# A squared-ReLU perceptron whose first matrix goes by seven quarter products in place of eight, in seven of eight feature groups

## The reference

```python
def squared_relu_mlp_2(h, w1, w2):
    return jnp.square(jax.nn.relu(h @ w1)) @ w2
...
        x = x + memory_xattn(rmsnorm(x, xa_ln[l]), rmsnorm(mem, xa_mem_ln[l]),
                             xa_wq[l], xa_wk[l], xa_wv[l], xa_wo[l])
        x = x + squared_relu_mlp_2(rmsnorm(x, ff_ln[l]), ff_w1[l], ff_w2[l])
```

## Time and profile before

| what | us |
|---|---|
| median of 3 runs (3623.42 to 3625.64) | 3624.16 |
| the profiled execution | 3652.24 |
| its span, first to last instruction | 3650.2 |
| PE busy in it | 3454.2 |
| DVE busy | 1768.0 |
| ACT busy | 1295.5 |

### The profile page before, as it was taken

One profiled execution on the slowest core, in us unless ns is written; L12 is line 12 of the kernel. 1 busy time (PEld: TensorE's weight loads), 2 busy tenths in 40 slices (PEclk: granted clock), 3 DMA queues, 4 the chain that ended last, 5 costly groups with the idle time before them and its releaser, 6 DMA issues. The chain is left out here.

```text
span 3650.2 us, 52599 instructions
## 1 busy us (share of the span) xinstructions
PE 3454.2 (95%) x21636; PEld 2817.0 (77%) x21636; DVE 1768.0 (48%) x2628; ACT 1295.5 (35%) x2096; POOL 159.2 (4%) x214
## 2 busy tenths in 40 slices
PE   7789899999999899999999989999999999999997
PEld 5687787788877587788877868788878767878886
DVE  5635653444444753444466354444452555444444
ACT  5223243322233743322234134432232574433221
POOL 0110000000000000000000200000000251000000
PEclk9899899999999999999999699999999999999998
DMA  3003131222231131222221023222232002222220
GB/s 145 23 4 108 59 137 51 89 96 99 93 107 58 40 134 56 91 96 92 92 83 54 2 81 116 70 85 100 92 119 75 36 2 94 104 78 96 92 92 35
DMA packets 42724, 289.78 MB, mean 79 GB/s; under 512 B 5475, under 2 KB 6243, under 8 KB 8860
## 3 DMA queue, kind: packets, MB, share of 16 engines
q1 hardware_dynamic: 42524, 286.92, 22.0%
HBM read 284.79 MB, written 2.12 MB: 79 GB/s over the span
## 5 line engine op out<-in xcount | busy, mean ns | idle before, releaser
L924 ACT ACTIVATE w_hi<-w_raw 128x2048 fp32r<-128x2048 f32 x112 | 214.8, 1918 | 861.6 <-PE ps L1044 445.7
L308 DVE TENSOR_TENSOR w_lo<-w_raw,w_hi 128x2048 fp32r<-128x2048 f32 x145 | 330.2, 2277 | 324.5 <-ACT w_hi L300 324.2
L1040 PE MATMUL ps<-a_x_hi,w_hi 128*128 128x512 f32 x1024 | 408.0, 398 | 7.5 <-PEq L270 7.5
L1041 PE MATMUL ps<-a_x_hi,w_lo 128*128 128x512 f32 x1024 | 405.7, 396 | 0.0
L1064 PE MATMUL ps<-mlp_u_lo,w_hi 128*128 128x512 f32 x1024 | 404.5, 395 | 0.0
L1065 PE MATMUL ps<-mlp_u_hi,w_lo 128*128 128x512 f32 x1024 | 404.5, 395 | 0.0
L1044 PE MATMUL ps<-a_x_lo,w_hi 128*128 128x512 f32 x1024 | 404.4, 395 | 0.0
L1063 PE MATMUL ps<-mlp_u_hi,w_hi 128*128 128x512 f32 x1024 | 404.4, 395 | 0.0
L414 PE MATMUL ps<-x_hi,w_hi 128*128 128x512 f32 x768 | 310.6, 404 | 24.4 <-PEq L270 17.0
L300 ACT ACTIVATE w_hi<-w_raw 128x2048 fp32r<-128x2048 f32 x145 | 274.9, 1896 | 96.5 <-PE ps L1065 41.0
L414 PE MATMUL ps<-x_hi,w_lo 128*128 128x512 f32 x768 | 308.3, 401 | 0.0
(11 more groups left out here) (568 smaller groups left out, 6121.6 us busy)
## 6 DMA issues: line engine op xcount, KB each, us to landing
w_raw<-in_weights SPq DMA_DIRECT2D x255, 1024.0 KB, 4.8
x_mem<-in_mem SPq DMA_DIRECT2D x4, 1024.0 KB, 4.9
hT<-in_x SPq DMA_DIRECT2D x1, 2048.0 KB
d_bias<-bias_rows SPq DMA_DIRECT2D x1, 2048.0 KB, 9.6
n_w<-in_cmp_w SPq DMA_DIRECT2D x1, 2048.0 KB, 7.5
out_h<-hT SPq DMA_DIRECT2D x1, 2048.0 KB, 6.3
t_xi<-in_ret_xi SPq DMA_DIRECT2D x1, 1024.0 KB, 7.2
w_raw<-in_weights SPq DMA_DIRECT2D x2, 512.0 KB, 3.3
```

The source lines that it names most:

```text
L308: dve.tensor_tensor(self.wlo[b % SPLIT][:, 0:width], self.raw[b % RAW][:, 0:width], self.whi[b % SPLIT][:, 0:width].bitcast(F32), ALU.subt ...
L924: act.activation(c.whi[b % SPLIT][:, :], c.raw[b % RAW][:, :], ACT.Copy).then_inc(c.hi_made.sem, 1)
L1040: pe.matmul(c.ps[:, t, :], whi[:, k, cols], x_hi[:, k, :], start=k == 0, stop=False)
L1041: pe.matmul(c.ps[:, t, :], wlo[:, k, cols], x_hi[:, k, :], start=False, stop=False)
```

## The change

For groups 1 to 7 the 512 x 1024 piece A of `w1` (transposed: features by k) and the 1024 x 512 tokens B are cut into 2 x 2 quarters: A into 256 features x 512 k, B into 512 k x 256 tokens. Before, the four quarters of the result took eight quarter products. Now they take seven (Strassen's algorithm in Winograd's form): of a11, a12 and a22, and of four sums of weight quarters (s1 = a21 + a22, s1 - a11 and so on), each with b11, b21, b22 or a difference of token quarters t1 to t4. A product is 2 tiles of 128 features x 4 k's x 3 = 24 matmuls of 256 tokens, both tiles in one bank.

- DVE makes the four sums of weight quarters (`mix`, L1153), 128x1024 each, mostly in place in `w_raw`. ACT and DVE then make hi and lo of each of the seven factors by half blocks (`step_part`, L1077 and L1161). The two blocks of a group held 4 halves; now there are 7.
- ACT copies the first product out of PSUM; DVE adds the products in seven additions of 128x512 (L1174), and relu (L1179) now reads SBUF, not PSUM.
- The token differences are made once in each perceptron (`MixedTokens`): ACT scales the 8 tiles of `hT`, DVE makes four differences, ACT and DVE their hi and lo parts. All of this is done while PE works on group 0's `hidden`, which stays as it was, or just behind.
- To make room in time, the squares of the norm move to the stage before, next to each addition to `hT` (`Squares`); only tile 7's stays. PE sums them after tile 0 and spreads the roots after tile 1.
- Half of the additions to `hT` (tiles 4 to 7) are queued in the next group, and two of the four raw slots are loaded again only after the last lo part of the group's first matrix.

```diff
+    def square(self, act, k):
+        if k >= 3:
+            act.wait_ge(self.added.sem, self.added.at(k - 2))
+        act.activation(self.place(k), self.c.hT[:, k, :], ACT.Square).then_inc(self.made.sem, self.made.up())
+    def add(self, dve, k):
+        dve.wait_ge(self.made.sem, self.made.at(k + 1))
+        self.c.link(dve, dve.tensor_tensor(self.total, self.total, self.place(k), ALU.add), self.added)
...
             self.ahead.lo_part(dve, t - 1)
+        if t >= 2:
+            self.ahead.squares.add(dve, t - 1)
         dve.tensor_tensor(c.hT[:, t, :], c.hT[:, t, :], psum, ALU.add).then_inc(done.sem, done.up())
...
+                self.ahead.squares.square(act, t)
...
+        low, high = slice(0, 4), slice(4, 8)
+        self.t1, self.t3, self.t2, self.t4 = (scratch[:, k, q] for k, q in ((low, FIRST), (low, SECOND), (high, SECOND), (high, FIRST)))
...
+        self.parts = [*zip(self.t_hi, self.t_lo), (x_hi[:, low, SECOND], x_lo[:, low, SECOND])]
+        plain = lambda k, q: (x_hi[:, k, q], x_lo[:, k, q])
+        self.operands = {"b11": plain(low, FIRST), "b21": plain(high, FIRST), "b22": plain(high, SECOND),
+                         "t1": self.parts[0], "t3": self.parts[1], "t2": self.parts[2], "t4": self.parts[3]}
...
+        for k in tiles:
+            act.activation(self.x[:, k, :], self.c.hT[:, k, :], ACT.Copy, scale=weight(k)).then_inc(self.scaled.sem, self.scaled.up())
...
+    def mix_first(self, dve):
+        dve.wait_ge(self.scaled.sem, self.scaled.at(4))
+        self.mix(dve, self.t1, self.t3, self.t1)
+    def mix_others(self, dve):
+        dve.wait_ge(self.scaled.sem, self.scaled.at(8))
+        dve.wait_ge(self.made.sem, self.made.at(1))
+        self.mix(dve, self.t3, self.t2, self.t3)
+        dve.wait_ge(self.made.sem, self.made.at(2))
+        self.mix(dve, self.t2, self.t2, self.t1)
+        dve.wait_ge(self.made.sem, self.made.at(3))
+        self.mix(dve, self.t4, self.t4, self.t2)
+    def hi_part(self, act, n):
+        act.wait_ge(self.made.sem, self.made.at(n + 1))
+        act.activation(self.parts[n][0], self.kept[n], ACT.Copy).then_inc(self.hi_ready.sem, self.hi_ready.up())
+    def lo_part(self, dve, n):
+        dve.wait_ge(self.hi_ready.sem, self.hi_ready.at(n + 1))
+        dve.tensor_tensor(self.parts[n][1], self.kept[n], self.parts[n][0].bitcast(F32), ALU.subtract).then_inc(self.lo_ready.sem, self.lo_ready.up())
...
-    ends, tiles = [], 0
-    for n in range(4 * G):
-        tiles += 2 if n < 2 or (n < 4 * G - 2 and n % 4 >= 2) else 4
-        ends.append(tiles)
+    ends = [2, 4]
+    for g in range(G - 1):
+        ends += [ends[-1] + n for n in (5, 7, 11, 15)]
+    ends += [ends[-1] + n for n in (4, 8)]
     c.tiles_end += [tile0 + n for n in ends]
+    steps = [(0, 0, "b11"), (0, 1, "b21"), (1, 0, "t2"), (1, 1, "t3"), (0, 0, "t4"), (1, 0, "t1"), (1, 1, "b22")]
+    SMALL = 5
...
+        room = sb("mlp_u", [P, 8, T])
+        u = room[:, 0:4, :]
...
+        s1 = room[:, 4:8, SECOND]
+        first_product = sb("mlp_product", [P, 2, HT])
+        sums = [sb("mlp_sum", [P, 2, HT])[:, :, :], room[:, 4:6, FIRST], room[:, 6:8, FIRST]]
...
+                a11, a12, a21, a22 = raw_quarter(n, 0), raw_quarter(n, 1), raw_quarter(n + 1, 0), raw_quarter(n + 1, 1)
+                return a11, a12, a21, a22, [(a11, 0), (a12, 0), (a11, 3), (a21, 2), (a22, 0), (s1, 1), (a12, 4)]
...
-                        sp.wait_ge(c.lo_made.sem, 4 * g + (b0 + j + 1))
+                        sp.wait_ge(c.lo_made.sem, 4 * g + (b0 + (1, 2, 4, 4)[j]))
...
+                def step_part(at, s):
+                    *_, sources = factors(2)
+                    source, mixed_before = sources[s]
+                    if s in (0, 1, 4):
+                        weights_landed(act, at, lambda g: 4 * g + (3 if s == 4 else 2))
+                    else:
+                        act.wait_ge(weights_mixed.sem, at(lambda g: weights_mixed.at(4 * g + mixed_before)))
+                    if s < 4:
+                        act.wait_ge(c.tile_done.sem, at(lambda g: tile0 + ends[4 * g + s // 2]))
+                    else:
+                        act.wait_ge(c.tile_done.sem, at(lambda g: tile0 + ends[4 * g + 1] + (1, 3, 4)[s - 4]))
+                    act.activation(slot_half(c.whi, s), source, ACT.Copy).then_inc(step_hi.sem if s < SMALL else c.hi_made.sem, 1)
...
-                    hi_part(at, lambda g: 4 * g + 3)
+                    step_part(at, 0)
+                    step_part(at, 1)
+                    if g == 0:
+                        u_part(0, at, 0, 0)
+                        u_part(0, at, 0, 1)
+                    step_part(at, 2)
+                    step_part(at, 3)
+                    if g == 0:
+                        act.wait_ge(c.tile_done.sem, tile0 + 4)
+                        mixed.hi_part(act, 3)
+                    if g:
+                        act.wait_ge(added.sem, at(lambda g: added.at(7 * g)))
+                    act.wait_ge(c.tile_done.sem, at(lambda g: tile0 + ends[4 * g + 1] + 1))
+                    act.activation(first_product[:, :, :], product(0), ACT.Copy).then_inc(copied.sem, 1)
+                    step_part(at, 4)
+                    if g == 0:
+                        u_part(0, at, 0, 2)
+                        u_part(0, at, 0, 3)
+                    step_part(at, 5)
+                    u_part(g + 1, at, 1, 0)
+                    step_part(at, 6)
                     hi_part(at, lambda g: 4 * g + 4)
-                    for t in (0, 1):
-                        u_part(g + 1, at, 1, t)
+                    u_part(g + 1, at, 1, 1)
                     hi_part(at, lambda g: 4 * g + 5)
-                    for t in (2, 3):
-                        u_part(g + 1, at, 1, t)
-                    hi_part(at, lambda g: 4 * g + 6)
+                    u_part(g + 1, at, 1, 2)
+                    u_part(g + 1, at, 1, 3)
...
+                norm.square_last(act)
                 c.make_hi(act, b0 + 1, BW)
-                norm.late_roots(act)
-                c.make_hi(act, b0 + 2, BW)
+                mixed.scale(act, range(4), norm.parts.weight)
+                norm.roots.root(act)
+                mixed.scale(act, range(4, 8), norm.parts.weight)
+                mixed.hi_part(act, 0)
+                mixed.hi_part(act, 1)
                 norm.late_row(act)
-                for t in range(4):
-                    u_part(0, first, 0, t)
-                groups(act, group, [(u_ready, 4), (u_hi_ready, 4)])
-                for n, b in enumerate((b0 + 4 * G - 1, b0 + 4 * G)):
-                    if b < len(c.blocks):
...
+                def add(at, n, out, a, b, step, known=0):
+                    dve.wait_ge(c.tile_done.sem, at(lambda g: tile0 + ends[4 * g + 1] + step + 1))
+                    if known:
+                        dve.wait_ge(added.sem, at(lambda g: added.at(7 * g + known)))
+                    dve.tensor_tensor(out, a, b, ALU.add).then_inc(added.sem, 1)
+                def relu_part(at, p):
+                    x, row = pieces[p]
+                    dve.wait_ge(added.sem, at(lambda g: added.at(7 * g + (1, 4, 5, 7)[p])))
+                    dve.scalar_tensor_tensor(x, x, 0.0, row, ALU.max, ALU.mult).then_inc(relu_ready.sem, 1)
...
+                    a11, a12, a21, a22, _ = factors(2)
+                    weights_landed(dve, at, lambda g: 4 * g + 2)
+                    weights_landed(dve, at, lambda g: 4 * g + 3)
+                    if g:
+                        dve.wait_ge(weights_mixed.sem, at(lambda g: weights_mixed.at(4 * g)))
+                    mix(at, 0, s1, a21, a22, ALU.add)
+                    mix(at, 1, a21, a11, a21, ALU.subtract)
+                    step_part(at, 0)
+                    step_part(at, 1)
+                    if g == 0:
+                        relu_tile(2)
+                        relu_tile(3)
+                    mix(at, 2, a11, s1, a11, ALU.subtract)
+                    if g:
+                        for t in range(4, 8):
+                            sum_part(at, t, lambda g: ends[4 * g - 1])
+                    step_part(at, 2)
+                    mix(at, 3, a12, a12, a11, ALU.subtract)
+                    step_part(at, 3)
+                    if g == 0:
+                        mixed.lo_part(dve, 3)
+                    step_part(at, 4)
+                    if g == 0:
+                        for t in range(4):
+                            u_part(0, at, 0, t)
+                    dve.wait_ge(u_lo_ready.sem, at(lambda g: u_lo_ready.at(4 * g + 4)))
+                    dve.wait_ge(copied.sem, at(lambda g: copied.at(g + 1)))
+                    add(at, 0, pieces[0][0], first_product[:, :, :], product(1), 1)
+                    relu_part(at, 0)
+                    if g:
+                        dve.wait_ge(added.sem, at(lambda g: added.at(7 * g)))
+                    add(at, 1, sums[0], first_product[:, :, :], product(2), 2)
+                    step_part(at, 5)
+                    if g == 0:
```

(56 more changed lines are left out.)

164 lines of the change are left out of this document (114 added, 50 removed).

## The result

| kernel | median, us | lowest and highest | runs |
|---|---|---|---|
| before | 3624.9 | 3623.42 to 3629.78 | 4 |
| after | 3569.76 | 3562.02 to 3573.89 | 4 |

The ratio is 0.9846, with a 95% interval of 0.9828 to 0.9863: faster by 55.1 us. The profiled execution of after took 3571.2 us, its span is 3569.3.

A forecast was written before the change was run, and what follows sets the result against it. PE was taken to bound the kernel, the loop's waits costing nothing. From a 3624.2 us median, 72.0 saved by products less 8 (first groups), 2.9 (barrier) and 4.6 (clock), or 56.5, gave 3567.7 us, range 3542 to 3598.

The forecast's parts named there:

- The product itself: PE's `hidden`: 168 matmuls of 256 tokens at 0.118 us take 19.82 us for 22.39, saving 72.0 us over 28 groups.
- rival 4: Weight loads on PE lie open, so 256-wide matmuls take as long as 512-wide: 470 us more, 4094 us; chance 0.02.
- ACT and DVE inside the loop: In each changed group DVE has 33.9 us, ACT 16.6; 1.4 us of cover at `back`'s first block, so no stall.
- The first group: First group of each perceptron: PE stalls 1.9 us ahead of the fifth product, behind DVE's second addition; 8 us in all.
- The stage before: One more addition of squares on DVE in front of the barrier before each perceptron: 4 x 0.72 = 2.9 us lost.
- The clock: PE half-clock episodes: 3.1 us behind new stalls plus 1.5 for later perceptron starts, together 4.6 us lost, bounds 0 and 9.
- The sum: Whole kernel: 72.0 - 8 - 2.9 - 4.6 = 56.5 us saved, giving 3567.7 us.
- 1: Products in `hidden` are faster, 0.1136 us a matmul: 77 us saved, 3547 us; chance 0.12.
- 5: The change does not do what it says: product waits on PE eat the 2.57 us, within 0.2% of 3624; chance 0.05.
- 2: DVE is late for `back`'s first block in every group, slipping 2.4 us: 28 us lost, 3596 us; chance 0.14.
- 3: DVE becomes the bound, operations on rows of 256 out of 512 costing more: 45.7 us a group, 3677 us; chance 0.05.

## Why the prediction was right

3567.7 was forecast, 3569.76 measured. Step by step:

- **The product itself**, 0.118 a matmul and 72.0 us in all: measured 0.1186 and 69.0. The row of the memory's keys in the slower layer was the right one to take. The reason given, that the 512-wide matmuls stand above 512 columns at 2.4 GHz too, chose the better row, but no run tests it as a cause. The faster layer (0.1136) has no counterpart here; the fastest products take 0.1167. The term was too high by 3.0 us. The loads of weights take 189 to 190 ns in after and are hidden under a distance of 119, as the earlier trace rows had it for the keys. The Trainium skill ("TensorE: Matmul & The Clock Gate", "Back-to-back issue gap") gives 262 cycles for 256 columns, as the gap of a matmul by itself, without the loads of weights that stand between all of these. By it an estimate is 0.109 us and a gain of 28 x 4.05 = 113 us; no product here ran like that, and the trace decides for 0.1186. For the loads, the prediction read the Trainium skill ("TensorE: Matmul & The Clock Gate", "The mechanism" in Part 3) too narrowly: beside differing row groups the section lets a load go ahead of running matmuls when it fills the background weight buffer, so rival 4 need not follow from it.
- **ACT and DVE inside the loop**, no stall: right, PE waits nowhere. DVE's 33.9 us are 32.1, ACT's 16.6 are 16.1. The cover of 1.4 us on `back`'s first block is 1.26, and the runs with spare additions show about how tight the place is: with one addition of 1.2 us PE doesn't wait, with a second it does.
- **The first group**, one stop ahead of the fifth product, 8 us: the place and the releaser are right; measured 4 x 2.27 = 9.1. The walk's two ends hold: PE was said to want the product at 35.6, and does (688.02 - 652.39 = 35.63), DVE's addition was said to end at 37.5 and ends at 690.03 - 652.39 = 37.64. Missing was the 0.26 us from the end of the addition to PE's first matmul. The 37.5 is partly luck: DVE starts its token differences at 9.55 in place of 10.4, and needs a microsecond more from there.

```profile
661.94 1.22 DVE L950 TENSOR_TENSOR mlp_u<-mlp_u 128x1024 f32<-128x1024 f32 x1 [1.62 <-ACT mlp_u L947]
```

- **The stage before**, 0.72 x 4 = 2.9: exact, and confirmed by the kernel with the moved norm alone. Its "no gain" from the eight squares less holds there too.
- **The clock**, 4.6 us: this is the term that was wrong. Its first half, 3.1 us behind the new stop, came in the profiled run as 2 x 1.5 = 3.0. Its second half took a start 0.72 us later to add a stretch; in after no start had one, so 3.0 us went away and the net was 0. In the six kernels that have both the stop of 2.27 and the idle time of 2.58 (after, the three with spare additions and the two with a wide t1), 13 of 24 starts had one and 5 of 24 stops, never both in one perceptron. That is 18 x 1.5 / 6 = 4.5 us a kernel, against 2 x 1.5 = 3.0 in the one profile of before, or 3.8 by the five of eight starts with the same idle time. By these the term should have been about 1 us, and no single run can give it.
- **The sum**: 69.0 - 9.1 - 2.9 - 0 = 57.0 in the two traces, 55.1 in the medians, 56.5 forecast. The errors are -3.0, -1.1, 0 and +4.6 us. They add up to 0.5: that the sum is this close is luck, since the clock's error cancels the first two. The two late places and the gain of about 70 us by the products don't rest on this luck.

Of the rivals, 1 (0.1136 a matmul), 4 (loads open) and 5 (the waits eat the gain) are refuted by the windows of `hidden`. 2, with DVE late in each group, did not come, but the spare additions show that it was near: it wanted a slip of 2.4 us, and 2.6 makes PE stand for 0.90 us. 3 rested on dearer operations with rows of 256 out of 512; they cost no more, 1221 ns against 1.22 by size. The groups of instructions of after:

```profile
L1153 DVE TENSOR_TENSOR w_raw<-w_raw 128x1024 f32<-128x1024 f32 x56 | 68.4, 1221 | 1.0
```
